# Moving the diagonal of reciprocal sums from VectorE to ScalarE in the attention pipeline of a two-layer encoder step

## What is computed

```python
h = rms_norm(x, ln_mix)
o = concat(fox_attend(...),      # 8 heads x 64, causal, with a cumulative decay
           swa_attend(...))      # 8 query heads x 64, window 128, a learned sink per head
x = x + o @ w_out
x = x + cross_attend(rms_norm(x, ln_mem), ...)   # 4 heads x 128, 256 memory tokens
x = x + conv_ffn(rms_norm(x, ln_ffn), ...)       # D_FF 2816
# in every attention: p = softmax(scores); o = p @ v
```

## Time and profile before

| | us |
|---|---|
| runs, median (lowest to highest) of 3 | 3662.82 (3659.05 to 3664.21) |
| the profiled execution | 3655.24 |
| its span in the trace | 3653.4 |
| busy: PE, DVE, POOL, ACT | 3391.1, 1879.3, 1201.9, 835.7 |
| mean granted clock of PE | 0.968 of full speed |

### The profile page before, as it was taken

How to read it: one execution, slowest core, us unless ns; L and a number is a source line. 1 busy time by engine, 2 the same in 40 slices (tenths; PEclk the granted TensorE clock), 3 DMA queues, 4 the chain that set the end, 5 groups by cost and what they waited for, 6 DMA issues and landing times. The chain is left out here.

```text
span 3653.4 us, 52717 instructions
## 1 busy us (share of the span) xinstructions
PE 3391.1 (93%) x21112; PEld 3257.3 (89%) x21112; DVE 1879.3 (51%) x3464; ACT 835.7 (23%) x1872; POOL 1201.9 (33%) x976
## 2 busy tenths in 40 slices
PE   6999997889999999999989999979989999999997
PEld 6988897778889999999978988878888999999997
DVE  5443444777664444443644443457766443444345
ACT  4331231434320000000232322224443100000001
POOL 4113112433343333333432122124233333333331
PEclk9999998999999999999999999988999999999998
DMA  4112112111111111111121111111111111111111
GB/s 145 39 43 58 42 37 64 56 43 39 30 41 44 43 45 44 44 46 45 41 70 51 39 42 59 46 43 61 44 35 32 41 44 44 44 44 44 45 44 63
DMA packets 85396, 175.65 MB, mean 48 GB/s; under 512 B 10416, under 2 KB 13744, under 8 KB 84752
## 3 DMA queue, kind: packets, MB, share of 16 engines
q1 hardware_dynamic: 71968, 132.90, 12.8%
q10 hardware_dynamic: 13184, 39.23, 3.7%
HBM read 150.36 MB, written 16.29 MB: 46 GB/s over the span
## 5 line engine op out<-in xcount | busy, mean ns | idle before, releaser
L613 POOL TENSOR_TENSOR WH<-RAW,zero 128x512 fp32r<-128x512 f32 x484 | 544.9, 1126 | 2366.1 <-PE PS L633 2353.6
L633 PE MATMUL PS<-HH,WH 128*128 128x384 f32 (+1 forms) x3312 | 872.0, 336 | 101.3 <-POOL WL L615 19.5
L633 PE MATMUL PS<-HL,WH 128*128 128x384 f32 (+1 forms) x3312 | 853.3, 330 | 0.0
L633 PE MATMUL PS<-HH,WL 128*128 128x384 f32 (+1 forms) x3312 | 852.6, 329 | 0.0
L633 PEld LDWEIGHTS PS<-HH,WH 128*128 128x128 f32 x3312 | 592.8, 190 | 123.4 <-POOL WL L615 22.5
L615 POOL TENSOR_TENSOR WL<-RAW,WH 128x512 fp32r<-128x512 f32 x484 | 661.4, 1367 | 37.9
L633 PEld LDWEIGHTS PS<-HL,WH 128*128 128x128 f32 x3312 | 595.4, 190 | 0.0
L633 PEld LDWEIGHTS PS<-HH,WL 128*128 128x128 f32 x3312 | 592.8, 189 | 0.0
L1686 DVE TENSOR_TENSOR XT<-PS,XT 128x320 f32<-128x320 f32 x448 | 303.3, 719 | 269.5 <-PE PS L633 269.3
L633 PE MATMUL PS<-G0H,WH 128*128 128x384 f32 (+1 forms) x960 | 288.1, 349 | 45.4 <-DVE XT L1530 29.4
L1115 ACT ACTIVATE PTH<-PS 128x512 fp32r<-128x512 f32 (+4 forms) x320 | 165.5, 520 | 681.3 <-PE PS L633 680.2
(11 more groups left out here) (249 smaller groups left out, 5087.9 us busy)
## 6 DMA issues: line engine op xcount, KB each, us to landing
RAW<-in_slabs SPq DMA_DIRECT2D x484, 256.0 KB, 2.7
XR<-decays ACTq DMA_DIRECT2D x16, 512.0 KB, 5.8
XT<-in_xT SPq DMA_DIRECT2D x8, 544.0 KB, 8.1
XR<-decays ACTq DMA_DIRECT2D x16, 272.0 KB, 7.0
out_fk<-T ACTq DMA_DIRECT2D x8, 544.0 KB, 2.7
out_fv<-T ACTq DMA_DIRECT2D x8, 544.0 KB, 2.8
out_y<-YT ACTq DMA_DIRECT2D x8, 544.0 KB, 3.2
RX<-ST ACTq DMA_DIRECT2D x16, 136.0 KB, 2.4
```

The source lines that it names most:

```text
L613: pool.tensor_tensor(WH[:, s, :], RAW[:, s, :], zero[:, 0:1].to_broadcast([128, HALF]), ALU.add).then_inc(w_hi, 1)
L633: ins = pe.matmul(*a, **k)
```

## The change

The reciprocal stays on DVE and now signals rc_ready. DVE's wait for its own completion, its DG instruction (one for both blocks, 128x256, or one of 128x128) and its wait on p_used at the end of a pipeline go. ACT makes DG, one 128x128 scaled copy per block, behind the exponentials of the following step and ahead of the outputs' high part.

```diff
+        rc_ready = sem("rc_ready")
...
                         ins.then_inc(e_ready, 1)
+                    if 1 <= s < n + 1:
+                        act.wait_ge(rc_ready, place.at("step", s))
+                        for h in range(steps[s - 1]["heads"]):
+                            ins = act.activation(DG[:, (s - 1) % 2, h, :], ident[:], ACT.Copy, scale=RC[:, (s - 1) % 3, h:h + 1])
+                        ins.then_inc(p_ready, 1)
                     if s >= 3:
                         act.wait_ge(o_full, place.at("step", s - 2))
...
                     h = st["heads"]
-                    if j + 1 >= n:
-                        dve.wait_ge(p_used, place.at("step", j + 2))
-                    wait_own(dve, dve.reciprocal(RC[:, k, 0:h], SM[:, k, 0:h]))
-                    if h == 1:
-                        ins = dve.tensor_scalar(DG[:, j % 2, 0, :], ident[:], RC[:, k, 0:1], None, ALU.mult)
-                    else:
-                        ins = dve.tensor_tensor(DG[:, j % 2, :, :], ident[:].unsqueeze(1).to_broadcast([128, 2, 128]),
-                                                RC[:, k, :].unsqueeze(2).to_broadcast([128, 2, 128]), ALU.mult)
-                    ins.then_inc(p_ready, 1)
+                    dve.reciprocal(RC[:, k, 0:h], SM[:, k, 0:h]).then_inc(rc_ready, 1)
```

## The result

| us | before | changed |
|---|---|---|
| runs, median (lowest to highest), 5 each | 3659.80 (3659.05 to 3664.21) | 3691.09 (3689.41 to 3709.36) |
| the profiled execution | 3655.24 | 3696.30 |
| its span | 3653.4 | 3694.5 |
| mean granted clock | 0.968 | 0.967 |

The changed kernel takes 1.0093 times as long, 95% interval 1.0069 to 1.0118: 34 us more, between 25 and 43 (the two medians alone are 31.3 us apart). Forecast were 3691 us and a loss of 28. So what follows reads the profiles for places and mechanisms, and the ratio for the size.

A forecast was written before the change was run, and what follows sets the result against it. PE, busy 93% of the span, bounds the kernel, so each positive DG lateness is lost time. 6.4 + 2.0 + 12.8 + 6.8 = 28.0 us on 3662.8 gives about 3691 us, range 3671 to 3711.

The forecast's parts named there:

- the clock, which it had put into a rival: New waits close together in memory attention cause two to four more half-clock stretches; with longer ping-pong 10 to 20 us; 14%.
- The price of a copy: Each 128x128 scaled copy on ACT takes 0.39 us, bounded by 0.28 and 0.50; two blocks usable after 0.83 us.
- the cheaper copy: With 0.28 us per copy instead of 0.39, the same latenesses add up to 17 us (3680).
- Fox: Fox, 13 steps in each of 8 pair runs: DG late by 0.8 us per pair, 6.4 us in all.
- First transposes: Very first transposes of a layer: DG 0.9 us late, 1.1 in layer 1, 2.0 us together.
- Memory attention: Two places, near 894 and 930, where DG comes late: 6.4 us per layer, 12.8 in two.
- Window attention: Steps at 694, between 721 and 734, and the last two: 3.4 us per layer, 6.8 in two.
- in each round: Window attention, 721 to 734: DG's 0.6 us goes into each DVE-ACT round, lengthening 1.6 to 2.3 us.
- VectorE's relief at nothing: What goes from DVE (0.43 us, its completion wait, some 0.2, per step) was costed at nothing.
- The faster one: DG leaves DVE's queue and PE's 20.2 us of waits on it vanish: 3643 us; chance 7%.
- slower by more: More half-clock stretches plus longer ping-pong wherever sample queries are taken add 10 to 20 us: about 3705; chance 14%.
- About 45 us and over 50 times: Sign of being right: PE's waits on DG name ACT, most in fox and memory attention, with this total and count.

The follow-up runs named there:

- dve_kept_busy: Changed kernel, with DVE still doing an instruction of DG's form where it made DG, in all but the first 13 steps: 3694.02 us, ratio 1.0107.
- ahead_early_recip: Against the kernel before: DG on ACT ahead of the following step's exponential, DVE's reciprocal moved forward to behind the first pass: 3654.06 us, ratio 0.9998.
- end_of_turn: Against the kernel before: DG on ACT behind the outputs' high part, last in its own step's turn, DVE's reciprocal moved forward: 3651.55 us, ratio 0.9995.

## Why the prediction was right

The mechanism holds: DG waits behind the following exponential, and the lateness reckoned for each step comes out in the trace. That the time, 3691, was met to a tenth of a microsecond is partly luck. It was added to 3662.8, a median of three executions; five gave 3659.8, and the loss was 31 (medians) to 34 us (ratio) instead of 28. What the sum left out are small waits in the fox and window parts, and the clock, which it had put into a rival.

- **The price of a copy** was right: 0.388 us against 0.39, two of them 0.68 us, so 0.29 us from one start to the next, and the sum 0.83 us from the last read to PE holds to 0.01 us in the fox step shown. The interval of 25 to 43 us excludes the 17 us of the cheaper copy. By the overhead that the page Perfetto Trace Analysis of the Trainium skill states in its section Optimizing Scalar/DVE Operations it would also have been near 17, with an estimate of 0.20 us of ScalarE per copy; the trace does not agree, at 0.29.
- **Fox.** The latenesses are as reckoned (0.32, 0.23 and 0.24 in a pair for 0.32, 0.24 and 0.24). Missed were one more step of the same pair that loses 0.22 us and a few that lose 0.04 to 0.08, so that a pair loses 1.15 to 1.2 instead of 0.8, and a half-clock stretch that lies longer over two of four pair borders (1.2 to 1.4 us each). 7.5 us in layer 0 instead of 3.2. In layer 1 the sum is only 1.5, because the profiled execution of before had a stretch at half clock there (last section); the other three pairs lost 2.70, 1.33 and 1.19.
- **First transposes.** 0.96 for 0.9 in layer 0. In layer 1 PE waits 1.23 us for DG, 1.1 predicted; the rest of the 3.65 goes with a longer time at the lower clock in the projections ahead, where nothing was changed (by the trace's clock records 30.0 us against 20.3).
- **Memory attention.** The mechanism was right to a tenth of a microsecond per step. The term was mis-sized by 1.5 to 3 us per layer, since the waits of 2.35 and 2.83 us at the end of its two dense places cost clock as well: the step behind each lost 1.3 to 1.5 us, in both layers.
- **Window attention.** The four steps between 721 and 734 lost 0.45, 0.02, 0.17 and 0.81 for 0.45, 0.16, 0.69 and 0.30: right in sum (1.45 for 1.6), not in each. The step at 694 lost 1.23 for 0.5, the last three 1.14 for 0.6, and two at 762 and 768 lost 1.6 together that were not reckoned, much the same in both layers. The totals are 2.6 and 6.5 us in the two layers for 3.4 each; in layer 0 the granted clock over the stage was 0.94 against 0.93, which gave some of the loss back. The runs with idle copies show that part of this loss is the occupancy of the round, as the 0.6 us "in each round" had said.
- **VectorE's relief at nothing** fits this kernel, as far as `dve_kept_busy` can tell. It is not shown for a kernel in which DG is in time: in `ahead_early_recip` the relief, the early reciprocal and the waits on DG that are gone together offset some 10 us of occupancy.
- **The rivals.** The faster one fell for the reason given: DG on ScalarE is never stretched, as the page SBUF — State Buffer of the Trainium skill, section Who interferes with whom, has it (384 to 401 ns here, 424 to 1479 on VectorE), and that decides nothing while DG waits behind an exponential. `end_of_turn` adds that even with all waits on DG gone the time stays where it was before: PE waits next for the outputs' low part and for ML. Of "slower by more" a part came true: some 7 us more than reckoned at the fox borders of layer 0 and in memory attention. Over the whole span the stretches at half clock add up to 249 us in the trace of the changed kernel and to 236 in that of before, of which 14 are the single stretch told in the last section. Without that one the changed kernel has 27 us more of them, which cost at most half, some 13 us: an estimate, since the half is lost only where PE was busy.
- **What would show it.** "About 45 us and over 50 times": the matmuls' row counts 40.5 us in 36 waits, the weight loads' 51.4 us in 55.

## What to carry to other kernels

An engine that is idle 77% of the time is no free place: what counts is what stands ahead of the moved instruction in its queue, measured from the last instruction ahead of it to the moment the consumer wants the result. The same instructions on the same engine cost 34 us behind the exponential (37 with the early reciprocal) and nothing measurable at the end of the turn, so a move between engines should be tried at each place in the turn, together with the producer of its input. Count a wait that disappears as a gain only after reading what the consumer waits for next.

## What was not expected of the hardware

- The lower clock follows single waits, not only the ends of stages: after 2.35 us (at 920.83) and 2.83 us (at 951.80) without work PE was granted about half its clock, while the waits of 0.93 to 1.38 us before them, in the same stage, left it at full clock.
- PE is also put at half clock where it never stood still. The view by windows of the kernel before, second fox pair of layer 1:

```profile
2040.00:2050.00 10.00, 10.00 (x74) 8.81 (x72) 5.65 (x17) 4.39 (x12) 0.00 (x0) 1.00 0.01 2
2050.00:2064.00 14.00, 14.00 (x60) 13.04 (x60) 5.53 (x15) 4.00 (x11) 0.00 (x0) 0.51 0.00 1
```

PE is busy without a gap in both, 74 matmuls in the first 10 us, 60 in the next 14. Such a stretch, of 13.7 us, is in 5 of the 14 profiled executions (twice in one of them), each time at another place of the fox part, and is worth some 5 to 6 us. All five are of the seven profiles with DG on VectorE, none of the seven with DG on ScalarE. With one profile of nearly every kernel that may be chance or not; what brings the stretch is open. Differences by stage of a few microseconds were believed here only where both layers show them.
